# The bias canvas's gaps filled from GpSimd's queue earlier: in the first mixer in place of the plain feed-forward

## What is computed

```python
# end of the first mixer, then the plain feed-forward
y = jnp.concatenate([out_a, out_b, out_c], axis=-1) @ w_out[l]
x = x + rmsnorm(y, norm_post_mix[l])
h = rmsnorm(x, norm_pre_ffn[l])
f = jnp.square(jax.nn.relu(h @ w_ff1[l])) @ w_ff2[l]
x = x + rmsnorm(f, norm_post_ffn[l])
...
# sliding-window attention: a bias by bucketed distance, and a band mask
bias = rel_bias[t5_bucket(dist)].astype(jnp.float32)
scores = scores + bias
valid = (rel >= 0) & (rel < WINDOW) & (blk * BLOCK + si - BLOCK >= 0)
scores = jnp.where(valid[None, :, None, None], scores, NEG)
```

## Time and profile before

| | |
|---|---|
| median of 3 runs | 1287.52 us (1287.12 to 1295.24) |
| the profiled execution's own time | 1294.2 us |
| its span, first to last instruction | 1292.3 us |
| mean granted clock of TensorE | 0.983 of full speed |
| busy: TensorE, VectorE, ScalarE, GpSimd | 95%, 69%, 47%, 12% |
| L871, the four fills, start | 158.31, 204.78, 254.13, 303.90 us |

### The profile page before, as it was taken

How to read it: one execution, slowest core, us unless ns; L and a number is a source line. 1 busy time by engine, 2 the same in 40 slices (tenths; PEclk the granted TensorE clock), 3 DMA queues, 4 the chain that set the end, 5 groups by cost and what they waited for, 6 DMA issues and landing times.

```text
span 1292.3 us, 17727 instructions
## 1 busy us (share of the span) xinstructions
PE 1229.9 (95%) x6966; PEld 1056.9 (82%) x6966; DVE 889.1 (69%) x1084; ACT 610.9 (47%) x786; POOL 155.9 (12%) x164
## 2 busy tenths in 40 slices
PE   7898899999899999979999999999999879999998
PEld 7786799999688888867888888888888657888887
DVE  4985555565777666675876666877676575966675
ACT  6556443334544443575544434444444585544342
POOL 4430212102310000250100000100001330100000
PEclk9998899999999999999999999999999889999999
DMA  9673269695685555452556554656553313555530
GB/s 311 204 197 122 88 151 234 175 239 149 158 301 194 194 182 180 161 159 86 177 194 195 181 182 158 204 193 195 182 168 133 106 35 100 192 192 181 183 128 33
DMA packets 163369, 219.60 MB, mean 170 GB/s; under 512 B 13693, under 2 KB 141761, under 8 KB 163181
## 3 DMA queue, kind: packets, MB, share of 16 engines
q1 hardware_dynamic: 153324, 212.28, 52.2%
q0 software_dynamic: 9984, 6.49, 2.8%
HBM read 213.26 MB, written 5.25 MB: 169 GB/s over the span
## 4 chain that ended last, share of the span: by engine, by line
PE 87%; DVE 8%; ACT 3%; issue 1%; DMA 0%; SPq 0%; DVEq 0%; ACTq 0%
PE ps L284 26%; PE ps L256 14%; PE ps L258 14%; PE ps L257 14%; PE ps L286 13%; DVE w_lo L237 2%; PE ps L587 2%; PE ps L600 1%; PE ps L612 1%; ACT w_hi L230 1%; DVE arena L690 1%; DVE h_both L476 0%; ACT h_both L467 0%; DMA raw<-in_w_mem_kv 0%; DVE scratch L519 0%
## 5 line engine op out<-in xcount | busy, mean ns | idle before, releaser
L230 ACT CAST w_hi<-raw 128x2048 fp32r<-128x2048 f32 (+3 forms) x198 | 374.1, 1890 | 436.5 <-PE ps L286 273.9
L237 DVE TENSOR_TENSOR w_lo<-raw,w_hi 128x2048 fp32r<-128x2048 f32 (+3 forms) x195 | 441.9, 2267 | 173.4 <-ACT w_hi L230 172.6
L284 PE MATMUL ps<-h_both,w_hi 128*128 128x512 f32 x1408 | 498.7, 398 | 4.6 <-DVE h_both L476 4.6
L286 PE MATMUL ps<-h_both,w_lo 128*128 128x256 f32 x1408 | 394.6, 280 | 0.0
L284 PEld LDWEIGHTS ps<-h_both,w_hi 128*128 128x128 f32 x1408 | 264.5, 188 | 70.6 <-issue 5.5
L286 PEld LDWEIGHTS ps<-h_both,w_lo 128*128 128x128 f32 x1408 | 265.7, 189 | 1.4
L256 PE MATMUL ps<-w_hi,act_hi 128*128 128x512 f32 x480 | 188.3, 392 | 1.4 <-DVE act_lo L1084 1.4
L258 PE MATMUL ps<-w_hi,act_lo 128*128 128x512 f32 x480 | 187.4, 390 | 0.0
L257 PE MATMUL ps<-w_lo,act_hi 128*128 128x512 f32 x480 | 187.2, 390 | 0.0
L291 DVE TENSOR_REDUCE arena<-ps 128x512 f32<-128x1024 f32 x88 | 107.8, 1224 | 82.1 <-PE ps L286 81.8
L362 POOL TENSOR_SCALAR rstd<-sums 128x1 f32<-128x1 f32 (+1 forms) x24 | 25.5, 1061 | 735.4 <-ACT scratch L351 656.4
(11 more groups left out here) (246 smaller groups left out, 1316.2 us busy)
## 6 DMA issues: line engine op xcount, KB each, us to landing
raw<-in_ffn_wg SPq DMA_DIRECT2D x44, 1024.0 KB, 5.4
raw<-in_ffn_wu SPq DMA_DIRECT2D x44, 1024.0 KB, 5.3
raw<-in_ffn_wd SPq DMA_DIRECT2D x44, 1024.0 KB, 4.8
raw<-in_w_ff SPq DMA_DIRECT2D x32, 1024.0 KB, 18.6
raw<-in_a_w_in SPq DMA_DIRECT2D x5, 1024.0 KB, 5.3
raw<-in_w_in SPq DMA_DIRECT2D x4, 1024.0 KB, 6.4
raw<-in_w_out SPq DMA_DIRECT2D x4, 1024.0 KB, 6.3
raw<-in_a_w_out SPq DMA_DIRECT2D x4, 1024.0 KB, 5.5
```

The costliest lines, as they stand in the source:

```text
L230: nc.scalar.copy(w_hi[:, place(b), 0:n], raw[:, b % RAW, 0:n]).then_inc(hi_ready, 1)
L237: nc.vector.tensor_tensor(w_lo[:, place(b), 0:n], raw[:, b % RAW, 0:n], w_hi[:, place(b), 0:n].bitcast(F32), ALU.subtract).then_inc(lo_rea ...
L284: nc.tensor.matmul(ps[:, bank + f, :], hi[:, k, f * P:(f + 1) * P], h_both[:, k, :, :].rearrange("p a b -> p (a b)"), start=k == 0, stop=F ...
L286: last = nc.tensor.matmul(ps[:, bank + f, 0:TOK], lo[:, k, f * P:(f + 1) * P], h_both[:, k, 0, :], start=False, stop=k == KD - 1, skip_gro ...
```

## The change

`canvas_fill()` is called in front of `add_normed_pool(0)`, right behind the two masks of the forget table, and no longer behind `norm_pool(2)`. Everything else is the same.

```diff
                                     base=0, pattern=[[0, H1], [-1, P]], channel_multiplier=1).then_inc(decay_ready, 1)
+            canvas_fill()
             add_normed_pool(0)
             if "F0" in STAGES:
                 norm_pool(2)
-                canvas_fill()
                 add_normed_pool(1)
```

## The result

Slower, clearly: 1396.48 us in the median of 4 runs (1391.96 to 1399.85) against 1291.38 us for the kernel before (1287.12 to 1295.36). The ratio is 1.080, with a 95% interval of 1.0767 to 1.0833. The profiled execution took 1399.38 us, 105.2 us more than the profiled one of before. 1354 was forecast, 1338 to 1370 as the range; the direction and the path by which the time is lost were right, the size was not. The first rival gave 1398.

What follows compares the result with a forecast made beforehand. TensorE, busy 95% of the span, was taken as the bound; add_normed_pool(0) waiting behind the fills would cost 66 us plus 0.5 us of clock, 66.5 us on the median 1287.52: 1354 us, range 1338 to 1370.

Steps and rivals of the forecast that it cites:

- The first rival: GpSimd's fills in the mixer keep their old cadence, 145.6 us for three waits: +110.3 us, 1398 us; chance 0.08.
- nothing is gained behind the fills or in the feed-forward: Plain feed-forward and GpSimd's queue there: removing the fills' traffic gains 0, upper bound 1 us.
- One DMA engine: GpSimd's fills: with 127 partitions as first dimension, each runs on a single DMA engine, share 0.06 to 0.07.
- a DMA share above 0.1 in the quiet stretch: Sign named in advance: seen while TensorE waits for the fills, it would overturn the single engine; 0.06 was expected.
- 512 KB at 22 GB/s is 23.8 us: Data time of one fill on its DMA engine, 23.8 us.
- the cadence of 31.5 us: Distance between fill starts on GpSimd: 6.7 us issuing, 23.8 us data, about 1 us to begin and report.
- The row of 22 GB/s: Windows 188:194 and 252:254 of the feed-forward, read as a fill nearly alone: share 0.06 to 0.07 at 22 GB/s.
- the split of the 46.47 us: First distance between fills in the feed-forward: 6.8 us issuing, 23.8 us data, 15.9 us left for weight loads sharing the engine.
- GpSimd gets on with another large DMA only when the fill before it is through: GpSimd's queue: each large DMA waits for the previous fill to finish; a tiny one goes out at once.
- VectorE under GpSimd's issuing: Attention beside the first fill: 6.8 us of issuing beside VectorE's masking, taken as 0, at most 6.8 us.
- the second rival: GpSimd's fills are quicker, 25.8 us each from 25.5 us to landing: +42 us, 1330 us; chance 0.06.

Runs made afterwards that it cites:

- e2: The kernel before (fills in the plain feed-forward), with each fill written from 128 partitions in place of 127: 1293.24 us against 1293.16, ratio 1.0005.
- e1: The changed kernel, with each fill written from 128 partitions in place of 127: 1289.84 us against 1293.16 for the kernel before, ratio 0.9974.
- e3: The changed kernel, with 125 partitions in each fill and the last two rows written by one more DMA behind norm_pool(2): 1294.99 us, ratio 1.0013.
- e5: The changed kernel, with the same gaps in eight fills of half the size in place of four, still 127 partitions: 1364.1 us, ratio 1.0541.
- e6: The changed kernel, with each fill cut in two along the rows: same bytes, twice as many rows, 8 DMAs of 1016 rows: 1498.68 us, ratio 1.1581.
- e4: The changed kernel, with only the first of four fills in the mixer and the other three behind norm_pool(2): 1297.49 us, ratio 1.0032.
- e7: e4 with L704 of the mixer's ten heads as tensor_tensor with the factor broadcast, in place of tensor_scalar: 1292.02 us, ratio 0.999.

## Why the prediction was wrong

- **Slower, and by which path: right.** add_normed_pool(0) stands behind the fills, TensorE does nothing from 151 to 251, and everything after moves with it. That nothing is gained behind the fills or in the feed-forward was right too (e2).
- **One DMA engine: right.** e1 and e3 show it by the number of partitions (e3 adds one small DMA), and the sixteen steps of `canvas_filled` show fifteen early and one late. The prediction's own sign against it, a DMA share above 0.1 in the quiet stretch, did come: 0.18 early in each fill. It is no second engine at work on the data, but the small packets of e5. In 158:242 of the changed kernel they are nearly all there is:

```profile
DMA packets 4096, 1.17 MB, mean 14 GB/s; under 512 B 3842, under 2 KB 3842, under 8 KB 4096
```

- **The failed step: "512 KB at 22 GB/s is 23.8 us", and the cadence of 31.5 us built on it.** Measured: 37.8 us from issuing to the next start, where the sum had 24.8 with its 1 us to begin and report, and 44.4 us. The data term was too small, and it had nothing in it for the rows: near 20 us are bytes and near 17.8 us the 1016 rows (e6). The three cadences were short by 9.0, 12.9 and 13.0 us, together 34.9 of the 42.5 us that were missing. The rest is 2.5 us of later masks (106.05 for 103.5), 3.9 us by which the median of before had moved, and 1 us of small terms.
- **How it came about.** The row of 22 GB/s was taken where I believed a fill to be alone. The windows had 0.06 to 0.07 and 22 GB/s, and the fill alone has 0.06 and 18: a load's tail ran beside it (0.03 of the 0.13 MB in 188:194). The trace of before held a warning: in 166:169, early in the first fill and with no load beside it, it moved 14 GB/s at a share of 0.18. And the split of the 46.47 us into issuing, data and loads had a free term (how much of the 0.45 MB came in time), which took up whatever was left. The balance closed, and proved nothing.
- **The rival with the right number had 0.08.** "For it: the three distances are alike." It should have weighed more: 46.47, 49.35 and 49.77 us were the measured thing; the 31.5 us were a model. As it turned out the loads of the feed-forward cost a fill 2 to 5 us, not 16, and the three loads beside the first fill in the changed kernel 2.6 us, not 6.5. That the rival's 1398 comes within 2 us is in part luck: its three waits are 145.6 us and the measured ones 135.9, and the later masks and the moved median of before made up for most of the 9.7 us.
- **What a fill waits for: wrong in form.** "GpSimd gets on with another large DMA only when the fill before it is through" holds for these fills only because the rows of one take nearly all the room of the queue (e3, e5, e6). For the forecast it made no difference.
- **VectorE under GpSimd's issuing: priced at 0, measured 4.8 us on one instruction, 4.5 in e4.** The text had bounded it by 6.8 us and said that it costs nothing as long as the fills end last; so it was. In e4, where they don't, TensorE waits 3.2 us.
- **The 25.5 us of the second rival: a misreading of the view** by two DMAs on one semaphore, as shown above; the prediction was right to distrust it.

## What to carry to other kernels

Look at the partition count of a DMA that is issued by GpSimd before moving it: with 127 in place of 128 the fills held the queue for 143 us in place of 4, at a sevenfold issuing time, and the row that could be added was never read. When a queue's instructions have a measured cadence, keep that as the forecast, until a row taken where nothing else runs says otherwise; check with the bytes of the neighbour queue that nothing else does. And what may stand in front of a due instruction is not only what is busy: 27 us of busy time held this queue for 143.

## What the runs showed that was not expected

- The time of a DMA on one engine depends on its rows nearly as much as on its bytes. Half the bytes at the same 1016 rows save only 10 of 37.8 us, and the fifteen engines that carry no data need 14 to 17 us for their four bytes a row.
- A DMA from GpSimd that uses fewer than sixteen engines here puts four bytes for every row on the others too. So rows on one engine use up room on all.
- GpSimd's time to issue rises with the rows on the fullest engine (worked out from the partitions), not with the rows as a whole: 0.92, 1.74, 4.55 and 6.67 us with 64, 200, 508 and 1016 rows on it, for 1024, 1000, 508 and 1016 rows in all. Half the bytes change nothing (6.66 us in e6).
- Two transfers that each use one engine can run beside each other (e5: 31 GB/s).
- tensor_scalar on float32 in SBUF stood still for up to 4.8 us under GpSimd's issuing and ended 0.1 us after the DMA's issuing; tensor_tensor did not stand still (e7).
- The view's time to landing is wrong where two DMAs in flight raise the same semaphore (25.5 us for 45).
